# Tile 1's front in another order on TensorE, the output projection and the second norm by halves, and the other tiles' tokens transposed in the norm's gap

## What is computed

```
xn = rmsnorm(x, norm1)
z  = einsum('btd,dn->btn', xn, w_in)           # 1024 -> 3912: aq af ai ag bq bk bv iq ik iw
group A: f = lb + (1-lb)*sigmoid(af); S_t = diag(f_t) S_{t-1} + (1-f_t) i_t^T; o_t = S_t^T silu(aq)
         a_out = rmsnorm_head(o) * silu(ag)
group B: q, k = rope(rmsnorm(bq)), rope(rmsnorm(bk)); score = sum_h w_h relu(iq_h . ik)
         softmax attention over the top-k keys by score
h = x + concat(A, B) @ w_o
y = h + peer(rmsnorm(h, norm2))                # per token: 8 heads x 16 of 16384 experts
peer: s = xn @ wq . subkeys; top 16 of each half, top 16 of their sums -> eidx, g = softmax
      out = sum_k g_k * gelu(xn . u[eidx_k]) * v[eidx_k]
```

## Time and profile before

| | us |
|---|---|
| median of 3 runs | 1263.51 (1260.94 to 1264.93) |
| the profiled execution, its device time | 1264.69 |
| its span, first to last instruction | 1262.9 |
| PE busy | 1099.1 (87%) |
| DVE busy | 807.8 (64%) |
| POOL busy | 732.6 (58%) |
| ACT busy | 344.7 (27%) |
| first gather issued by POOL | 142.91 |

### The profile page before, as it was taken

The page is one execution under the profiler, slowest core; times in us unless marked ns, Lnnn a source line. Parts: engine busy times, 40 slices in busy tenths (PEclk is TensorE's granted clock), DMA queues, the critical chain, the costliest instruction groups (busy, mean ns, idle before and its releaser), DMA issues. The chain is left out here.

```text
span 1262.9 us, 12585 instructions
## 1 busy us (share of the span) xinstructions
PE 1099.1 (87%) x3549; PEld 551.5 (44%) x3549; DVE 807.8 (64%) x2015; ACT 344.7 (27%) x782; POOL 732.6 (58%) x774
## 2 busy tenths in 40 slices
PE   6978999999999799887889999999677777788888
PEld 2765756556554354333435534534222222222233
DVE  1452799595876674949984666578667656764430
ACT  3521212532412223323331322322122222221111
POOL 0000356655666665767675766677576767777753
PEclk9988899999999899999998999999899999999999
DMA  8743499999999999999999999999999999999996
GB/s 350 315 172 152 164 416 412 412 336 328 383 374 359 404 409 402 410 398 383 410 406 388 409 409 409 408 409 408 413 409 410 410 409 410 408 409 404 409 344 233
DMA packets 126356, 470.68 MB, mean 373 GB/s; under 512 B 14664, under 2 KB 17744, under 8 KB 124112
## 3 DMA queue, kind: packets, MB, share of 16 engines
q0 software_dynamic: 110592, 402.70, 81.1%
q1 hardware_dynamic: 15696, 67.19, 13.5%
HBM read 465.34 MB, written 4.42 MB: 372 GB/s over the span
## 5 line engine op out<-in xcount | busy, mean ns | idle before, releaser
L1643 PE MATMUL PSUM<-UV,DIAG 128*128 128x512 f32 x1536 | 741.5, 617 | 116.8 <-DMA UV<-in_p_v,EIDX 113.9
L1244 DVE CUSTOM_DVE_ANT_0 UV<-UV,PSUM 128x1024 f32<-128x1024 f32 x384 | 462.8, 1218 | 216.5 <-DMA UV<-in_p_u,EIDX 211.7
L506 POOL DMA_INDIRECT UV<-in_p_u,EIDX x384 | 369.4, 962 | 292.4 <-DVE EIDX L1057 141.5
L1643 PEld LDWEIGHTS PSUM<-UV,DIAG 128*128 128x128 f32 x1536 | 275.0, 192 | 521.0 <-DMA UV<-in_p_v,EIDX 275.6
L514 POOL DMA_INDIRECT UV<-in_p_v,EIDX x384 | 362.3, 944 | 224.8 <-PE PSUM L1643 98.7
L843 ACT ACTIVATE DIAG<-CST,WGT 128x128 f32<-128x128 f32 x384 | 152.1, 400 | 723.2 <-PE PSUM L1643 719.9
L1283 PE MATMUL PSUM<-WR,XW 128*128 128x512 f32 (+1 forms) x128 | 50.6, 555 | 0.0
L1292 PE MATMUL PSUM<-XW,WR 128*128 128x256 f32 x192 | 42.3, 379 | 0.0
L1292 PEld LDWEIGHTS PSUM<-XW,WR 128*128 128x128 f32 x192 | 36.5, 190 | 6.7 <-issue 1.8
L1283 PEld LDWEIGHTS PSUM<-WR,XW 128*128 128x128 f32 x128 | 24.2, 190 | 25.2 <-issue 22.5
L1244 DVE DVE_READ_ACCUMULATOR2_ANT DOTS<- 128x1 f32 x384 | 31.6, 82 | 0.0
(11 more groups left out here) (220 smaller groups left out, 856.8 us busy)
## 6 DMA issues: line engine op xcount, KB each, us to landing
UV<-in_p_u,EIDX POOLq DMA_INDIRECT x384, 10.8
UV<-in_p_v,EIDX POOLq DMA_INDIRECT x384, 10.8
WR<-in_p_wq SPq DMA_DIRECT2D x10, 512.0 KB, 7.0
UV<-in_w_B SPq DMA_DIRECT2D x2, 2048.0 KB, 12.5
UV<-in_w_o SPq DMA_DIRECT2D x2, 2048.0 KB, 8.0
UV<-in_p_wq SPq DMA_DIRECT2D x2, 2048.0 KB, 7.8
WR<-in_w_B SPq DMA_DIRECT2D x2, 2048.0 KB, 10.0
XW<-in_w_o SPq DMA_DIRECT2D x8, 512.0 KB, 6.8
```

The lines of the kernel that those rows point to most:

```text
L506: nc.gpsimd.indirect_dma_start(UBUF[n % RU], None, a["p_u"], bass.IndirectOffsetOnAxis(EIDX[:, n:n + 1], 0)).then_inc(u_got[n % RU], 16)
L1244: v.tensor_tensor_reduce(out=row, in0=row, in1=XNP, scale=1.0, scalar=0.0, op0=ALU.mult, op1=ALU.add, accum_out=DOTS[:, i % 2, s:s + 1]).t ...
L1643: ins = mm(bank[6 + k][:, :], DIAG[:, n % ND, :], VBUF[n % RV][:, k * 512:(k + 1) * 512], start=False, stop=False)
```

## The change

- **PE's order in the front of tile 0.** `qp` follows `fp` directly; `ti`, `tk` and `tq` follow it. `vp` is cut into two halves over the contraction (weights' rows): four products, then `dt`, `ke` and `at`, then the other four. `gp` is cut by heads: two heads, then the outer products of blocks 0, 2, 1, 3 (`FIRST_BLOCKS` is reordered), then the other two. Then come `lg`, the other outer products, `inner_out` and `state_out` of blocks 1 to 5, `pt`, `state_out` of blocks 6 and 7, `pv`, `ss`.
- **The output projection by halves of columns.** `mixed` gets a parameter `halves`; the four products with `MIXB` are made for columns 0 to 511 and then for 512 to 1023, and the same for `MIXA`, so that bank `wo` 0 is complete four products ahead of `wo` 1.
- **The second norm of tile 0 by halves.** ACT squares each half when its residual is added (`halves_sq`), DVE scales the first half's sum in between (`half_sum`), DVE norms in two halves, and PE transposes and queries by halves. The square's output goes to `XN2[1]`.
- **The tokens of tiles 2 and 1** are transposed after `wo` and ahead of `x2`. Their normed tokens lie in `XN2[0]` and `WQ[1]` instead of `WR`; DVE waits for `xt` of tile 2 before it writes `XN2[0]`. ACT evicts them after the first head's scores, and DVE's copy `XNP` moves behind the choice of the first two heads.
- **ACT's order**: `log_f`, `exps` and `qp` ahead of `out_kq` and `out_dots`; `gp` ahead of the numerators; `square_o` ahead of `pv`. **DVE's**: `keys` ahead of `scores`, `end_keys` ahead of `pick`, two updates ahead of the maxima, `normalise` after update 6.
- **SP**: chunk B0 is loaded in two DMAs of half the columns, with a semaphore each; O0 and O1 are issued ahead of the stores of the new keys.

```diff
-FIRST_BLOCKS = (0, 2, 4, 6, 1, 3, 5, 7)
+FIRST_BLOCKS = (0, 2, 1, 3, 4, 6, 5, 7)
...
+        if name[0] == "xt" and name[1]:
+
+            b = 8 - 2 * name[1] + name[2]
...
-        XN = view(WR, 0, NT, D)
+        XN = [WR[:, 0:D], WQ[1].rearrange("p c n -> p (c n)"), XN2[0]]
...
-            load_first("B0")
+
+            for k, landed_ in enumerate((b0_in, w_in_slot[0])):
+                cols = slice(k * WCOLS // 2, (k + 1) * WCOLS // 2)
+                sp.dma_start(UV[:, cols], a["w_B0"][:, cols]).then_inc(landed_, 16)
...
-            store_new(0)
             take(sp, ("fp", 0))
             load_first("O0")
+            take(sp, ("qp", 0))
+            load_first("O1")
+            store_new(0)
...
+                    for n in range(2):
+                        cols = slice(n * 512, (n + 1) * 512)
+                        stored(act, ("wo", 0, n))
+                        own.done(nc.scalar.activation(XN2[1][:, cols], X[0][:, cols], ACT.Square, accum_out=SMALL[:, 69 + n:70 + n]),
+                                 halves_sq)
+                    act.wait_ge(half_sum, 1)
+                    own.done(nc.scalar.activation(SMALL[:, 9:10], SMALL[:, 70:71], ACT.Sqrt, bias=SMALL[:, 71:72], scale=1.0 / D), std2)
...
-            out_xt(1)
-            out_xt(2)
+            log_f(0)
+            exps(0)
+            copy_out(("qp", 0), SQ[0], heads4, func=ACT.Silu)
             out_kq(0)
-            log_f(0)
             for par in range(2):
                 out_dots(0, par)
-            exps(0)
-            copy_out(("qp", 0), SQ[0], heads4, func=ACT.Silu)
             copy_out(("vp", 0), AIV[0])
+            copy_out(("gp", 0), SG[0], heads4, func=ACT.Silu)
...
+            first(CHOICES[0] + 3)
+            out_xt(2)
+            out_xt(1)
             first(-1)
...
             sums_of_logs(0)
+            keys(0)
             scores(0, 0, IH)
+            end_keys(0)
             hidden(0)
-            keys(0)
...
+            update(0, 0)
+            update(0, 1)
             maxima(0, 0, 0)
             maxima(0, 1, 0)
-            for b in range(8):
+            for b in range(2, 7):
                 update(0, b)
-                if b == 3:
-                    normalise(0)
+            normalise(0)
+            update(0, 7)
...
-            for t in (1, 2):
-                pe.wait_ge(xn_ready, t + 1)
-                for g in range(2):
-                    transposes(("xt", t, g), [XN[:, t, (4 * g + c) * P:(4 * g + c + 1) * P] for c in range(4)])
+            channels_of(("qp", 0), XNT2, weights("AQ"), range(4))
             keys_queries(0)
-            index_dots(0)
-            channels_of(("qp", 0), XNT2, weights("AQ"), range(4))
-            rows_of(("vp", 0), XNT2, weights("AI"))
-            keys_and_dots(0)
+            w = weights("AI")
+            pb = start(("vp", 0))
+            for c in range(KC):
+                if c == KC // 2:
+                    index_dots(0)
+                    keys_and_dots(0)
+                ins = mm(pb[:, :], XNT2[:, c, :], w[:, c, :], start=c == 0, stop=c == KC - 1)
...
-            for c in MIXED:
-                mixed(0, c)
+            for n in range(2):
+                for c in MIXED[0:4]:
+                    mixed(0, c, (n,))
+            for n in range(2):
+                for c in MIXED[4:8]:
+                    mixed(0, c, (n,))
+            for t in (2, 1):
+                pe.wait_ge(xn_ready, t + 1)
+                for g in range(2):
+                    transposes(("xt", t, g), [XN[t][:, (4 * g + c) * P:(4 * g + c + 1) * P] for c in range(4)])
```

92 lines of the change are left out of this document (55 added, 37 removed).

## The result

The changed kernel takes 1258.27 us (median of 20 runs, 1254.16 to 1261.97), the kernel before in the same set 1264.51 (20 runs, 1260.43 to 1267.96): a ratio of 0.995, 95% interval 0.9937 to 0.9964. That is 6.2 us faster, where 16 us were forecast. The sign was right, the size was not: the measured time lies 3.8 us above the upper end of the range. The profiled execution of the changed kernel took 1260.99 us, 2.0 more than its span of 1259.0.

A forecast was written before the change was run, and what follows sets the result against it. The kernel was taken as a serial front of 143 us plus an untouched 1120 us loop. First gather 16.1 us earlier, TensorE's later units some 17.5, less 0.4 for XNP: 16 us off, forecast 1247.5 us, range 1238 to 1254.5.

The forecast's parts named there:

- The front to the logits: later by 3.5 us: TensorE's front up to the logits: reordered work, 18.2 us from the dots on, ends them at 74.3 instead of 70.75.
- The second outer products: at the same time: Behind the logits: they wait for DVE's update 2 instead of the numerators, and start at 76.4 against 76.47 before.
- From there to the end of `wo`: 33.1 us: Second outer products to the output projection's end: 33.1 us instead of 44.7, without `gp` and two waits, ending at 109.5.
- `wo` to first gather: 17.3: Output projection's end to first gather: 17.3 us instead of 21.7, through norm, transposes and query by halves and a filled gap.
- the bound of 19.6: Output projection's end to first gather: 19.6 us if TensorE does not stay at 2.4 GHz.
- B0 in two DMAs: nothing: Loads at the front's start: splitting chunk B0 costs 0 us, bounds 0 and +0.5.
- XNP behind two choices: +0.4: DVE's copy ahead of the loop's first dot product: costs 0.4 us, bounds 0 and 1.23.
- The loop as before: From first gather to the end: 1120 us as before, its work untouched and shifted by the front's gain.
- half clock in new places: Rival: gaps at 54.8 and 76 bring low clock, state products and tail slow too; 5.9 us, time 1253.4, chance 0.13.
- 2.3 for the tail: Term of the half-clock rival: the stretch from the output projection to the first gather takes 2.3 us more.
- Full clock in the whole front: Rival: state products and their neighbours in the front run at full clock; 7.4 us less, time 1240.1, chance 0.15.

The follow-up runs named there:

- gp_last: The changed kernel with the gate projection whole behind the second outer products, as before the change; ratio 0.9954 to the kernel before.
- vpw_fill_quiet: The changed kernel with the value projection in one piece and three unread 512-column products ahead of the second outer products; 1249.34 us, ratio 0.989 to the kernel before.
- tail_only: The kernel before with only the front's end changed (halved output projection, norm and query, moved transposes, XNP behind choices); old order up to the squares; ratio 0.9931.
- b0_whole: The changed kernel with chunk B0 loaded in one DMA, as before the change; one run, 1258.50 us.

## Why the prediction was wrong

The first gather was forecast at 126.8 us and came at 136.06. The 9.3 us, step by step as the prediction put them:

- **"The front to the logits: later by 3.5 us"**: short by 3.2. The chain of ACT was right: TensorE reached the dots at 55.66 (forecast 56.1) after idling 1.94 us (1.3), and DVE had the penalty in time. But the 18.2 us from there were taken from rows at full clock, and a low stretch of 6.8 us follows the wait: the dots took 2.66 us (1.7), `ke` and `at` with their transposes 1.0 more than forecast, the second half of `vp` 4.62 (3.5). The outer products took 2.05 (1.2) at full clock, as their row holds for the old order of the blocks. The logits end at 77.5, not 74.3.
- **"The second outer products: at the same time"**: the mechanism was right (they wait for DVE's update, 2.30 us, where 2.1 were forecast); they start at 79.8, 3.4 us later, as the logits are late.
- **"From there to the end of `wo`: 33.1 us"**: this is the step that failed most, 38.2 us (from 79.82 to 118.06). The outer products took 3.67 (2.1), the state products 8.55 and 3.43 (8.85 for all), `pt` 1.95 (1.0), `pv` 2.88 (2.0); the rest was 0.8 shorter. That the waits for `pt` and for the squares go was right, and so was the cover of `mix_a`. Two things were wrong. The 2.1 us of the outer products were a row at the low clock already; the 1.6 on top are not the clock's but come with the new block order, which the prediction did not price. And the other rows of before were carried over with their clock. Before, the 8.70 us of `gp` stood between the outer products and the state products. Windows of the kernel before:

```profile
74.00:81.50 7.50, 5.03 (x47) 4.83 (x48) 2.69 (x10) 2.20 (x10) 0.00 (x0) 0.54 0.01 2
81.50:91.00 9.50, 7.09 (x65) 6.86 (x65) 6.59 (x21) 3.07 (x4) 0.00 (x0) 1.00 0.28 90
91.00:98.00 7.00, 7.00 (x54) 6.58 (x51) 0.00 (x0) 0.60 (x1) 0.00 (x0) 0.76 0.45 180
```

  The clock was back at full from 81.5 on, within `gp`, and `pt`, half of the values and much of the state products were measured at full clock. The change moved `gp` away, and no float32 product of 512 columns and no long train of products of 128 came between 77.5 and the squares at 101.83. `gp_last` shows the return within `gp`, `vpw_fill_quiet` shows 40 of the state records at 4.54 us once something dense precedes them (and the outer products at 2.06, which is their full-clock time in the new block order).
- **"`wo` to first gather: 17.3"**: right but for 0.7 us (18.0); the fill of the gap, the query at 2.02 and the norm by halves are all in the rows. The same stretch took 18.0 in `vpw_fill_quiet` and 19.6 in `tail_only`, where part of it was at the low level, as the bound of 19.6 had it.
- **"B0 in two DMAs: nothing"**: right. **"XNP behind two choices: +0.4"**: too small at its place, 3 us to the first `p_v` gather in the changed kernel, and with no effect on the time that could be measured.
- **The loop as before**: right within its scatter; over nine profiles of changed kernels on the chips where before takes 1263 to 1265 us it took 1115 to 1126 us from G to the end.

So of the 9.3 us about 7.3 are products at the low level that were priced wholly or in part at full clock, and 2.4 are the block order; 0.7 behind `wo` and 0.2 at the wait for the update come on top, and the rest, some 1.3 us, went the other way (TensorE was at the dots 0.4 earlier, and the squares and `wo` took 0.8 less).

Of the rivals, "half clock in new places" named both places, the gap at 54.8 and the one at 76, and the state products at the low level; it had 1253.4 and a chance of 0.13. Its sum is short in itself: it speaks of two places at 1.7 us each, but 1.7 + 1.9 + 2.3 = 5.9 counts only one; with both it would be 7.6 us and 1255.1. Its 2.3 for the tail did not come (18.0 us, at full clock), and the low stretches were longer than the 3.2 us that it gave each: 6.8 and 23.9 in the first profile. "Full clock in the whole front" was wrong for the reason that the prediction gave against it, the fall at 98.3 with TensorE busy. Its figure of 30 records in the 10.2 us behind 98.3 mixes products: it takes in the squares and the first `MIXB` products, which have 512 columns. The range was too narrow on the slow side: no case in it had the low level last from the second outer products to the output projection. The trace of before would have priced that: in the 5.1 us from 98.3 to 103.4, state products alone, it has 25 records at a clock of 0.50, 0.20 us each, so an estimate of 11.4 us for the 56, where the changed kernel took 8.55 and 3.43.

The forecast of 126.8 itself is reached, at 126.17, by `vpw_fill_quiet`, with L 6.8, but with the value projection whole and the filler; the order as forecast had 131.0 at best.

What stays open: why one execution of the same order has 20.5 us at the low level and another 30.7. The 20 times of the changed kernel spread over 7.8 us, those of the kernel before over 7.5, so they do not tell. Open too is where the loop makes up the start of 3 us, and what the old block order would give back in the changed kernel: by the rows above 2.4 us as it ran is an estimate, but the banks for which the second group waits follow from that order too, and no run tried it.

## What to carry to other kernels

A duration read from a row holds for the clock that was granted there and for the products that ran ahead of it. When a change moves dense products away from between sparse ones, put a case into the range in which the sparse ones are at the low level until the next dense products come, or leave something dense there: here three products of 512 columns that nobody reads, in a gap of 3 us, took 7.2 us off the time together with undoing a cut. A new order of small products is a term of its own, even when nothing is added: the outer products took 1.75 times as long. Measure the parts of a change apart, but count what the clock did in each profile before a difference is given to an edit: the tail alone had 5.1 of the 6.85 us here, and 1.6 of them were the clock's.

## What the runs showed of the hardware

- With TensorE busy 27.73 of 28 us, the granted clock was 0.57 behind 2.6 us of products of 16 columns and 0.88 behind 2.8 us of products of 512 columns.
- The time at the low level in one and the same order was 20.5 (three times), 27.3 and 30.7 us in five executions, and the time from the forget gate to the first gather moved with it: 95.9 to 96.0, 98.9 and 101.3 us.
- Sixteen outer products (32 records of 32x128) took 1.17 us at full clock and 2.09 at the low one when four in turn read four groups of 32 rows, and 2.05 and 3.67 to 3.79 us when they read two.
- The low level ended within `gp` in `gp_last` (at 84 us) and in the kernel before (at 81.5), and in the changed kernel only at 104, behind the squares; in `b0_whole` it also ended for 3 us at 85, within products of 16 columns.
- A switch of ACT's table cost 1.28 us and no more behind it, as in the earlier trace rows: the function starts 1.30 us after the load does. The Trainium skill's drain of 1.38 us ("ScalarE: Activation LUTs", what ACT_TABLE_LOAD costs) was not seen in the changed order either.
- On two of the chips the kernel before took 1365 and 1368 us instead of 1263 to 1265; the unaltered changed front took the same time there (G - F 101.39 against 101.33, L 30.7 in both).
